# The queue order around DeltaNet's block substitution, and the substitution on VectorE instead of GpSimd

## What is computed

```python
g = jnp.cumsum(g, axis=-1)
decay = jnp.exp(jnp.where(incl, g[..., :, None] - g[..., None, :], -jnp.inf))
k_beta = k * beta[..., None]
a_mat = jnp.einsum("bhnid,bhnjd->bhnij", k_beta, k) * jnp.where(strict, decay, 0.0)
rhs = jnp.concatenate([v * beta[..., None], k_beta * jnp.exp(g)[..., None]], axis=-1)
sol = lax.linalg.triangular_solve(eye + a_mat, rhs, left_side=True, lower=True, unit_diagonal=True)
qk = jnp.einsum("bhnid,bhnjd->bhnij", q, k) * decay
q_dec = q * jnp.exp(g)[..., None]
def step(s, xs):
    v_new = u_c - jnp.einsum("bhck,bhkv->bhcv", w_c, s)
    o = jnp.einsum("bhck,bhkv->bhcv", qd_c, s) + jnp.einsum("bhij,bhjv->bhiv", qk_c, v_new)
    s = s * jnp.exp(gl_c)[..., None] + jnp.einsum("bhck,bhcv->bhkv", kd_c, v_new)
    return s, o
```

## Time and profile before

| | us |
|---|---|
| median of 3 runs | 3055.91 (3055.65 to 3061.22) |
| the profiled execution | 3061.32, its span 3059.6 |
| TensorE busy | 2888.3 (94%), mean granted clock 0.968 |
| VectorE, ScalarE, GpSimd busy | 1299.4, 1072.4, 1206.5 |
| DeltaNet, preparation of head 0 | 1247.4 to 1282.7 of the span |
| inversions of heads 0 to 3 begin at | 1282.7, 1372.2, 1468.95, 1567 |
| the last recurrence ends at | 1647 |

### The profile page before, as it was taken

One profiled execution on the slowest core, in us unless ns is written; L12 is line 12 of the kernel. 1 busy time (PEld: TensorE's weight loads), 2 busy tenths in 40 slices (PEclk: granted clock), 3 DMA queues, 4 the chain that ended last, 5 costly groups with the idle time before them and its releaser, 6 DMA issues. The chain is left out here.

```text
span 3059.6 us, 38554 instructions
## 1 busy us (share of the span) xinstructions
PE 2888.3 (94%) x15219; PEld 2356.4 (77%) x15219; DVE 1299.4 (42%) x1953; ACT 1072.4 (35%) x1829; POOL 1206.5 (39%) x805
## 2 busy tenths in 40 slices
PE   6999999999999969578778999999999999999998
PEld 5878787877888846477667887878888888888887
DVE  5233233321479949666564353322233232232323
ACT  4241313243044539455544122332333333333232
POOL 2222122121123320423421433466666666766663
PEclk9999999999999979878798999999999999999999
DMA  4434233343545357210103546332322333332331
GB/s 114 165 132 140 80 102 102 100 132 94 184 148 176 120 189 249 80 44 31 73 31 126 179 141 208 105 100 93 102 91 91 103 96 124 97 97 91 114 110 58
DMA packets 239571, 352.78 MB, mean 115 GB/s; under 512 B 32928, under 2 KB 186272, under 8 KB 239392
## 3 DMA queue, kind: packets, MB, share of 16 engines
q1 hardware_dynamic: 239392, 350.32, 35.2%
HBM read 263.71 MB, written 96.36 MB: 118 GB/s over the span
## 5 line engine op out<-in xcount | busy, mean ns | idle before, releaser
L102 PE MATMUL pj_acc<-u_hi,pj_w_hi 128*128 128x512 f32 x1464 | 576.6, 394 | 10.6 <-DVE u_lo L823 10.6
L2763 DVE TENSOR_TENSOR x_tm<-m_ps,x_tm 128x512 f32<-128x512 f32 x384 | 265.0, 691 | 745.8 <-PE m_ps L104 745.8
L104 PE MATMUL pj_acc<-u_hi,pj_w_lo 128*128 128x512 f32 x1464 | 571.9, 391 | 0.0
L103 PE MATMUL pj_acc<-u_lo,pj_w_hi 128*128 128x512 f32 x1464 | 571.7, 391 | 0.0
L551 POOL TENSOR_TENSOR pj_w_lo<-pj_w_raw,pj_w_hi 128x1024 fp32r<-128x1024 f32 x61 | 159.2, 2610 | 722.0 <-ACT pj_w_hi L600 722.0
L2645 POOL TENSOR_TENSOR m_lo<-gate,held 128x1024 fp32r<-128x1024 f32 x96 | 237.8, 2500 | 270.0 <-ACT held L2562 270.0
L102 PEld LDWEIGHTS pj_acc<-u_hi,pj_w_hi 128*128 128x128 f32 x1464 | 275.9, 188 | 85.7 <-issue 18.2
L104 PEld LDWEIGHTS pj_acc<-u_hi,pj_w_lo 128*128 128x128 f32 x1464 | 276.1, 189 | 58.2
L103 PEld LDWEIGHTS pj_acc<-u_lo,pj_w_hi 128*128 128x128 f32 x1464 | 276.2, 189 | 56.2
L102 PE MATMUL m_ps<-held 128*128 128x512 f32 x768 | 299.7, 390 | 2.4 <-DVEq L2744 2.4
L102 PE MATMUL m_ps<-held,m_h_hi 128*128 128x512 f32 x768 | 299.5, 390 | 0.0
(11 more groups left out here) (308 smaller groups left out, 4939.8 us busy)
## 6 DMA issues: line engine op xcount, KB each, us to landing
gate<-in_w_mlp_dram SPq DMA_DIRECT2D x48, 1024.0 KB, 5.4
gate<-in_w_mlp_dram SPq DMA_DIRECT2D x96, 512.0 KB, 3.7
proj<-pj_stage SPq DMA_DIRECT2D x61, 768.0 KB, 3.4
pj_w_raw<-in_w_in_dram SPq DMA_DIRECT2D x61, 512.0 KB, 5.2
gate<-proj SPq DMA_DIRECT2D x24, 768.0 KB, 4.4
mo_w_raw<-in_w_out_dram SPq DMA_DIRECT2D x48, 256.0 KB, 2.9
rpb_bias<-pj_shut SPq DMA_DIRECT2D x48, 192.0 KB, 3.1
rpb_bias<-rpb_near SPq DMA_DIRECT2D x24, 384.0 KB
```

Source lines behind the costliest of these rows:

```text
L102: pe.matmul(out, w_hi, x_hi, start=first, stop=False)
L103: pe.matmul(out, w_hi, x_lo, start=False, stop=False)
L104: return pe.matmul(out, w_lo, x_hi, start=False, stop=last)
L2763: dve.tensor_tensor(xt, ps2[:, q % 4], xt, ALU.add).then_inc(added, 1)
```

## The change

Word for word from the diff, without its least parts. It has these parts.

- `solve` moves from GpSimd's queue to VectorE's, cut in three: in steps 4, 5 and 6 of the recurrence, between `rb` and `st`.
- The query products of the last two units move from step 4 to step 5, the gate of z from step 5 to 6.
- The factor beta enters the exponentials as a logarithm (`lnb`, `sb`), so that the scores are one instruction of 128x512 and not four of 128x128. The logarithm is taken once, ahead of attention.
- The exponentials of the decay rows (`row_decays`) move from k = 0 and 2 of a head's own inversion to steps 5 and 6 of the recurrence before, on ScalarE.
- GpSimd makes the inclusive masks of the next head before the decayed queries of this one.
- ScalarE places two of the three forward units in `un`; VectorE's placing is 12 copies instead of 16, all behind `narrow`.
- The cutting of the blocks moves ahead of the output copies (ScalarE) and behind the state updates (VectorE).
- The columns of the next head move from k = 6 to k = 1; transposes, products and the output normalisation take other positions.

```diff
-SQUARES_AT, ROOT_AT, EG_AT, CEXP_AT = 1, 5, (0, 2), 10
-LENGTHS_AT, MEAN_AT, DIAG_AT, SPREAD_AT, NORM_AT, GATE_AT = 2, 3, 5, (7, 9, 11), (8, 10, 12), 12
-TURN_AT = (0, 3, 6, 9, 11, 13)
-TOKEN_AT = ((1, 2), (4, 5), (7, 8), (10, 11), (12, 13), (14, 15))
-COLUMNS_AT = 6
-INCL_AT = {8: 4, 11: 5, 13: 0, 15: 1}
+SUM_AT, SQUARES_AT, LENGTHS_AT, MEAN_AT, ROOT_AT, DIAG_AT = 0, 3, 4, 5, 7, 7
+SPREAD_AT, NORM_AT, GATE_AT = (9, 11, 13), (10, 12, 14), 14
+COLUMNS_AT, CEXP_AT = 1, 9
+TURN_AT = (0, 3, 6, 9, 12, 15)
+TOKEN_AT = ((0, 1), (3, 4), (6, 7), (9, 10), (12, 13), (15, 16))
+INCL_AT = {8: 4, 10: 5, 12: 0, 14: 1}
...
-INCL_END = {1: 3, 3: 2}
+INCL_END = {3: 3, 4: 2}
 AMAT_IN = {0: (4, 5), 1: (0, 1), 2: (3, 2)}
-QK_IN = {0: (4, 5), 1: (0, 1), 4: (3, 2)}
-CUT_IN, WIDE_IN, ZTANH_IN, ZGATE_IN, SPREAD_IN = 2, 3, 4, 5, 7
+QK_IN = {0: (4, 5), 1: (0, 1), 5: (3, 2)}
+CUT_IN, WIDE_IN, ZTANH_IN, ZGATE_IN, SPREAD_IN = 2, 3, 4, 6, 7
+EG_IN = (5, 6)
+SOLVE_IN = {4: (0, 4), 5: (4, 9), 6: (9, 14)}
...
             pool.sem_inc(S["mask_i"], NG6)
-            solve(0)
             place(0)
             for i in range(HEADS):
-                decayed_queries(i)
                 if i + 1 == HEADS:
+                    decayed_queries(i)
                     continue
                 pool.wait_ge(S["g_in"], (i + 1) * 32 + 32)
                 if i:
                     pool.wait_ge(S["o_mm"], i * 24)
                 for n in PREP:
                     masked(qk2[:, (i + 1) % 2, n], i + 1, n, incl).then_inc(S["mask_i"], 1)
+                decayed_queries(i)
                 for k, n in enumerate(ORDER):
                     pool.wait_ge(S["s_mm"], i * NS + 2 * NG6 + k + 1)
                     masked(am[:, n], i + 1, n, strict).then_inc(S["mask_s"], 1)
-                solve(i + 1)
                 place(i + 1)
...
+                for q in Q32:
+                    act.copy(by_direction(un, q, 0)[:, 0:NTB:2, :, q], compact(c1, q, 0)[:, 0:NTB:2]).then_inc(S["un0_d0"], 1)
+                act.wait_ge(S["spread"], 2 * i + 2)
                 for q in Q32:
                     act.copy(by_direction(tn, q, 0)[:, :, :, q], compact(c2, q, 0)).then_inc(S["tn0_act"], 1)
...
+                        if step in EG_IN:
+                            row_decays(i + 1, EG_IN.index(step))
...
-                for j in range(4):
-                    last = dve.scalar_tensor_tensor(am[:, n, j], ps[:, 4 + 2 * (GRAMS.index(tg) % 2), j],
-                                                    ncol2[:, i % 2, 2 + d, 4 * tg + j:4 * tg + j + 1], decays[:, j], ALU.mult, ALU.mult)
-                last.then_inc(S["am_done"], 1)
+                dve.scalar_tensor_tensor(am[:, n], ps[:, 4 + 2 * (GRAMS.index(tg) % 2)], -1.0, decays, ALU.mult,
+                                         ALU.mult).then_inc(S["am_done"], 1)
...
+            def solve(i, c, first, last):
+
+                both = [528, 2]
+                if first == 0:
+                    dve.wait_ge(S["wide"], i + 1)
...
+                    squares = [both, [32, 16], [1, 16]]
+                    c.link(dve.tensor_copy(strided(sol, 0, squares), strided(c2, 0, squares)))
+                    c.link(dve.memset(strided(sol, 0, [both, [33, 16]]), 1.0))
+                for j in range(first + 1, last + 1):
+                    n = 15 - j
+                    term = strided(part, 0, [[j * n, 2], [n, j], [1, n]])
+                    right = strided(sol, j + 1, [both, [32, j], [1, n]])
+                    c.link(dve.tensor_tensor(term, strided(sol, j, [both, [32, j], [0, n]]),
+                                             strided(c2, 33 * j + 1, [both, [0, j], [1, n]]), ALU.mult))
+                    c.link(dve.tensor_tensor(right, right, term, ALU.add))
...
-            def place(i, first):
...
+            def place(i):
+
+                for t, free in ((slice(1, NTB), 4 * BOTH), (slice(0, 1), 24)):
+                    if i:
+                        dve.wait_ge(S["new_mm"], (i - 1) * 24 + free)
+                    else:
+                        dve.wait_ge(S["cleared"], 4)
                     for q in Q32:
-                        dve.tensor_copy(by_direction(un, q, d)[:, t, :, q], compact(src, q, d)[:, t]).then_inc(S["un0"], 1)
+                        dve.tensor_copy(by_direction(un, q, 1)[:, t, :, q], compact(c2, q, 1)[:, t]).then_inc(S["un0_d1"], 1)
+                for q in Q32:
+                    dve.tensor_copy(by_direction(un, q, 0)[:, 1:2, :, q], compact(c1, q, 0)[:, 1:2]).then_inc(S["un0_late"], 1)
```

More of the change, by code:

```diff
@@ L1040, in attention @@
     strict, incl, join = masks
-    y2, gq, kb, col2, ncol2, cx2 = ahead
+    y2, gq, kb, col2, ncol2, cx2, lnb, sb2 = ahead
     dd0 = kb[:].rearrange("p (a j) n -> p a j n", j=4)
@@ L1675, in main @@
                         strict_decays(i + 1, STRICT_MID[step])
+                    if more and step == CUT_IN:
+                        cut_blocks(i + 1)
                     for j, d, t in live_chains(step):
@@ L1696, in _ @@
             act.sem_inc(S["exp_i"], NG6)
+            for d in range(2):
+                row_decays(0, d)
             cut_blocks(0)
@@ L1968, in main @@
                     if i:
+                        if k == SUM_AT:
+                            out_sum(i - 1)
                         if k == MEAN_AT:
@@ L2000, in main @@
                             dve.tensor_copy(st[:, j], ps[:, j, 2]).then_inc(S["st_ev"], 1)
+                    if more and step == CUT_IN:
+                        cut_blocks(i + 1)
                 if more:
-                    place(i + 1, False)
+                    place(i + 1)
                 c.end()
@@ L2006, in _ @@
             chains = [Chain(dve, S["chain"], i, K_DN) for i in range(HEADS)]
+            solving = [Chain(dve, S["solve"], i, SOLVE) for i in range(HEADS)]
             dve.memset(ps[:, 0:2], 0.0).then_inc(S["blank"], 1)
-            dve.sem_inc(S["chain"], 8)
-            chains[0].n = 8
+            dve.sem_inc(S["chain"], 9)
+            chains[0].n = 9
             dve.sem_inc(S["cols_in"], 1)
-            for part in range(STEPS):
-                prepare(0, part, chains[0])
-            place(0, False)
+            for step in range(STEPS):
+                prepare(0, step, chains[0])
+                if step == CUT_IN:
+                    cut_blocks(0)
+            place(0)
             for i in range(HEADS - 1):
```

93 lines of the change are left out of this document (39 added, 54 removed).

## The result

| | before | after |
|---|---|---|
| median of the runs | 3055.78 (3055.21 to 3061.22, 4 runs) | 3072.59 (3069.13 to 3075.16, 4 runs) |
| the profiled execution, its span | 3061.32, 3059.6 | 3075.16, 3073.4 |
| TensorE's mean granted clock | 0.968 | 0.962 |
| busy VectorE, ScalarE, GpSimd | 1299.4, 1072.4, 1206.5 | 1348.4, 1081.0, 1157.3 |

The ratio is 1.0049, with an interval of 1.0036 to 1.0062: the changed kernel is slower by 0.5%, 16.8 us. The forecast was 3064, the range 3042 to 3081. So the sign and the range held, and half of the size was missed. Which half is what the rest of this document is about. In the trace the operations of GpSimd are of two kinds here: the masks (L1523, 128x512, about 1.27 us each) and the query products (L1532, 128x1536, 3.4 us each).

The account below looks back on a forecast made before the run. No engine is full in DeltaNet, so waits between engines, read on VectorE, were taken to bound it. Preparation -5.2, recurrences +9.3, inversions +4, attention +0.6 gave +8.7, taken as +8 on 3055.9: 3064 us, range 3042 to 3081.

Parts of the forecast that it names:

- Preparation of head 0: Ahead of head 0's inversion: scores in one instruction and the substitution on VectorE save time, -5.2 us.
- Recurrences: Heads 0 to 2: a step with enough work takes that work plus 1.5 us; +3.1 each, together +9.3 us.
- The blocks: Inversion starts: GpSimd's operations hold up VectorE's small ones; 10.3 us late in head 0, 10.9 in heads 1 and 2.
- Transposes: Inversions: nearly all TensorE waits for VectorE's products before its transposes, 19.5 us over four heads, go: -4.9 a head.
- the old stall of the columns: Inversions: the columns' old hold-up at k=6 goes, -4.3 us at head 0, -4.5 with ScalarE's wait at heads 1 and 2.
- one level: Inversions: one level that TensorE did in advance during the new delay, -1.6 us per head.
- +2 for the clock: Inversions of heads 0 to 2: 2 us each added because TensorE's clock is low for a time after idling.
- the gates close behind the stall: Rival: TensorE, once let go, runs levels 1 and 2 at full clock; some -8 us, 3056, no change; chance 0.22.
- the clock stays down: Rival: TensorE stays at 0.50 behind each new stall; some +17 us, 3081, slower still; chance 0.15.
- the first rival: The no-change rival: levels 1 and 2 at full clock since the waits before the fall are removed; 3056, chance 0.22.
- Attention: Ahead of attention: ScalarE's logarithm and a new table for the exponentials, 0 to 1.3 us, taken as +0.6.
- the stalls at the start don't bind: Rival, inversion starts: GpSimd lets VectorE's small operations in between, or masks come later than its copies; 3040, chance 0.23.

Follow-up runs that it names:

- e2: The changed kernel with GpSimd's inclusive masks held until VectorE has placed its blocks: 3074.20 us (ratio 1.0054).
- e5: The changed kernel with the columns back at k = 6 and GpSimd's masks held until VectorE has placed its blocks: 3052.04 us (ratio 0.9985).
- e9: The changed kernel with GpSimd's masks for the next head held until VectorE has written that head's columns (k = 1): 3037.39 us (ratio 0.9935).
- e1: The changed kernel with the next head's columns back at k = 6 and their exponentials at k = 10: 3060.93 us (ratio 1.0006).
- e13: The changed kernel plus 64 unread TensorE products in the stall of heads 1 and 2, and sums of squares with 32 columns of ones: 3067.37 us (ratio 1.0038).
- e6: The changed kernel with the output normalisation and gate of the head before at their old positions: 3057.22 us (ratio 0.9997).
- e15: The kernel of e12 plus 16 unread TensorE products in heads 1 and 2, ahead of the second product of k = 4: 3032.04 us (ratio 0.9915).
- e3: The changed kernel with the substitution back on GpSimd, so the queue changes alone: 3060.41 us (ratio 1.0015).
- e10: The changed kernel with the edits of e9 and e3, so masks held behind the columns and substitution on GpSimd: 3028.49 us (ratio 0.9904).
- e4: The kernel before with only the substitution moved to VectorE's queue at steps 4 to 6: 3080.64 us (ratio 1.0072).
- e12: The kernel of e10 with the output normalisation's sums of squares taken with 32 columns of ones instead of 1: 3027.26 us (ratio 0.9904).

## Why the prediction was right, and where it was short

**Preparation of head 0**, -5.2: measured -5.6. The substitution was put at 8.1 us and takes 8.4; the price by the linked products of the earlier trace rows held. It is not the link that costs, though: an operation of 28 elements takes 0.19 us itself, and the next starts 0.03 behind its end. On GpSimd, with nothing beside it, the same work ran from 1264.74 to 1277.29 in the preparation of head 0 of the kernel before, 12.5 us. In head 1 it ran from 1449.35 to 1463.31, 14 us, of which 1.4 were lost at one sum of 0.4 us that met a VectorE product of 128x1536:

```profile
1264.74 0.61 POOL L1534 COPY dn_sol<-dn_c 128x512 f32<-128x512 f32 x1 [10.33 <-DVE dn_c L1905]
...
1277.04 0.26 POOL L1542 TENSOR_TENSOR dn_sol<-dn_sol,dn_part 128x28 f32<-128x28 f32 x1
```

```profile
1455.61 1.81 POOL L1542 TENSOR_TENSOR dn_sol<-dn_sol,dn_part 128x112 f32<-128x112 f32 x1
```

Alone, GpSimd is 1.5 times as long, short of the factor of about 2 of the Trainium skill (GPSIMD Engine Reference, 4.1 Engine selection).

**Recurrences**, +9.3: measured +3.0, +2.1 and +2.3, that is 7.4. Steps 4, 5 and 6 were forecast at 4.05, 5.9 and 5.95 us; they are 4.13, 5.69 and 6.28. The rule "work and 1.5 us" held.

**The blocks**: forecast k = 0 of head 0 at N + 19.5 (measured 19.5), k = 2 of heads 1 and 2 at N + 24.6 (25.5 and 25.0), k = 1 of head 3 at N + 17.4 (1592.99, N + 17.7). The mechanism was read out of the kernel before, where three rows are held up by a mask and the fourth is not (the prediction counts four), and e2, e5 and e9 confirm it: in e9, with GpSimd held back, every one of these operations has its ordinary price.

**Transposes**, -4.9 a head: TensorE's waits of 19.5 us ahead of them (L1723) are gone from the list of waits; no run shows by itself what they were worth in time.

**The terms that failed** are those set against the blocks: "-4.9", "the old stall of the columns", "one level" and "+2 for the clock". For N to R, all told, I had +2.7, +1, +1 and -0.5, sum +4. Measured, from the ledger: -5.1, +14.4, +5.2 and +0.4, sum +14.9. The gross delays were right to a microsecond; what came back behind them was not. I took it as a fixed amount, 7.6 us in head 0 and 9 to 10 in heads 1 and 2. It was 16 in head 0 (45.1 us from k = 2 to R became 29.0), and in heads 1 and 2 it was -2.6 and +5.9. The difference goes with TensorE's granted clock, 0.97 there and 0.58 and 0.73 here. So both of my rivals on the clock came in, one in each place: "the gates close behind the stall" in head 0, "the clock stays down" in heads 1 and 2, and the sum of the two lies between their 3056 and 3081.

In head 0 the term that was too small is the one for the old stall of the columns, -4.3. The stall at k = 0 did not bring the 16 us back: e9 has no stall and is as quick there. Moving the columns from k = 6 to k = 1 was worth 10.4 us of head 0 with the stall (e1 against the changed kernel) and 11.1 without (e5 against e9), because the clock no longer fell behind k = 6. That is the reason which the first rival gave, that the change removes the waits ahead of the fall. In heads 1 and 2 the same move is worth 0.3 and -3.1 us (e5 against e9).

The range was held partly by luck. Head 0 came out 7.8 us better than its term and heads 1 and 2 together 17.6 us worse; without head 0's error in the other direction the time would have been near 3080 (3072.6 + 7.8), at the edge of the range.

That the clock is cause and not company is shown in part. e13 adds work to TensorE's stall, removes none, and the levels behind it get shorter, by 11 and 4.4 us against the changed kernel's one profile and by 2.8 at the least against all stretches of this kind. e6 leaves the stall and gets the same levels in 27 us at 0.94, but 5.3 us of its gain are the sums of squares that run in the stall's shadow. e15 shows the limit: clock that is bought with work in the path is worth what it costs.

**Attention**, +0.6: DeltaNet starts 2.7 us earlier. 1.4 of that is there at 611 us, in a part of the program that the change does not touch, so it is a difference between two executions. The rest I did not find.

**What each part costs**, by medians. The substitution on VectorE: 23.3 us on the kernel before, 13.5 on the queue changes (e3), 8.9 where nothing is blocked (e10 against e9). My terms for it, +3.65 a recurrence and -3.3, make +7.7, which is the last case: there it is nearly all in the recurrences. What it costs above that in the other two is not its own time. In e4's head 3 a part is where it moves VectorE's other work against GpSimd's; the rest is a lower clock, and whether the move brought that is not shown. The queue changes alone: +3.3. With one wait more they bring 28.8 us, so the gain that they are able to give was there, and the meeting of the masks with placing and columns took it. My rival "the stalls at the start don't bind" priced a kernel without the stalls at 3040; e9 gives 3037. That is near by luck in part, for the rival had no term for head 0's clock.

**Still open**: why the clock falls at about N + 18 in heads 1 and 2 in e9, e10 and e12 and not in head 0 (e12 excludes the one-column products), why a wait of TensorE of 1.2 us at k = 6 (e1) goes with the fall there and one of 0.4 does not, and why equal queues give 37.8 us or 44.3 for the same levels. The scatter of the profiled executions is of that size, 6 us a head, so the ledger's columns k = 2 to k = 17 are to be read with it; the medians of the runs suffer less from it.
